# Layer norms split over three engines, high parts multiplied first, and out products moved into the attention's last pairs

## What is computed

```python
for l in range(DEPTH_2):                       # 2 layers
    proj = h @ w_in[l]                         # 8 "in" units
    ...                                        # conv, rotary keys, gating: o_a, o_c
    o_b = blocked_attention(q, k, v, ...)      # 4 heads each, no mask
    o_d = blocked_attention(q_full, k_full, v_d, ...)
    mix = jnp.concatenate([o_a, o_b, o_c, o_d], axis=-1) @ w_out[l]
    h = layer_norm(DEEPNORM_ALPHA * h + mix, ln_mix_g[l], ln_mix_b[l])
    up = depthwise_conv(h @ ffn_w_up[l], ffn_conv_w[l], ffn_conv_b[l])
    f = (jax.nn.silu(up[..., :D_FF]) * up[..., D_FF:]) @ ffn_w_down[l]
    h = layer_norm(DEEPNORM_ALPHA * h + f, ln_ffn_g[l], ln_ffn_b[l])
```

## Time and profile before

| | |
|---|---|
| median of three runs | 2215.06 us |
| profiled execution | 2213.04 us, span 2211.2 us |
| TensorE busy | 2074.5 us, 94% of the span |
| VectorE busy | 1194.1 us, 54% |
| ScalarE busy | 782.5 us, 35% |
| GpSimd busy | 164.4 us, 7% |
| chain that ended last | PE 79%, DMA 10%, DVE 6%, ACT 4%, issue 2% |

### The profile page before, as it was taken

How to read it: one execution, slowest core, us unless ns; L and a number is a source line. 1 busy time by engine, 2 the same in 40 slices (tenths; PEclk the granted TensorE clock), 3 DMA queues, 4 the chain that set the end, 5 groups by cost and what they waited for, 6 DMA issues and landing times.

```text
span 2211.2 us, 24796 instructions
## 1 busy us (share of the span) xinstructions
PE 2074.5 (94%) x10070; PEld 1450.8 (66%) x10070; DVE 1194.1 (54%) x1803; ACT 782.5 (35%) x1191; POOL 164.4 (7%) x120
## 2 busy tenths in 40 slices
PE   6999998999998899889998999999899989999997
PEld 5787787843333333358566888887685567888875
DVE  6455624423332233367775764656677847646565
ACT  4546534221111111154573421222445734212222
POOL 1000000000000000000200110102002001101020
PEclk9999999999999999999999999999999999999999
DMA  5342243479999999932201222233132012232321
GB/s 197 113 156 77 77 152 115 181 286 407 404 413 400 402 412 415 419 111 95 72 1 57 95 95 95 81 110 115 58 114 72 1 58 79 100 104 85 110 96 38
DMA packets 41138, 357.61 MB, mean 162 GB/s; under 512 B 6321, under 2 KB 7513, under 8 KB 13377
## 3 DMA queue, kind: packets, MB, share of 16 engines
q1 hardware_dynamic: 35872, 340.89, 40.6%
q0 software_dynamic: 4288, 10.95, 1.6%
q10 hardware_dynamic: 864, 4.19, 0.5%
HBM read 354.94 MB, written 6.83 MB: 164 GB/s over the span
## 4 chain that ended last, share of the span: by engine, by line
PE 79%; DMA 10%; DVE 6%; ACT 4%; issue 2%; SPq 0%; DVEq 0%; ACTq 0%
PE bank L1078 43%; PE bank L2007 10%; PE bank L443 7%; DMA ring<-in_expert_up_w 4%; PE bank L458 3%; DMA AUX<-in_expert_up_w 3%; PE bank L465 2%; PE bank L1799 2%; DMA H<-in_expert_up_w 2%; PE bank L1784 1%; PE bank L1815 1%; DVE split_weights L1285 1%; PE bank L2032 1%; PE bank L2100 1%; ACT S L1864 1%
## 5 line engine op out<-in xcount | busy, mean ns | idle before, releaser
L1078 PE MATMUL bank<-split_x_high,split_weights 128*128 128x512 f32 x2144 | 668.9, 392 | 22.8 <-DVE split_x_low L1299 14.7
L1078 PEld LDWEIGHTS bank<-split_x_high,split_weights 128*128 128x128 f32 x2144 | 405.5, 189 | 113.1 <-issue 28.7
L1293 ACT ACTIVATE split_weights<-ring 128x2048 fp32r<-128x2048 f32 (+2 forms) x117 | 218.8, 1870 | 554.1 <-PE bank L1078 519.4
L1285 DVE TENSOR_TENSOR split_weights<-ring,split_weights 128x2048 fp32r<-128x2048 f32 (+2 forms) x117 | 265.2, 2267 | 172.1 <-ACT split_weights L1293 172.0
L1078 PE MATMUL bank<-split_products,split_weights 128*128 128x512 f32 x1200 | 332.4, 393 | 4.5 <-DVE split_products L1475 4.5
L1078 PE MATMUL bank<-split_x_low,split_weights 128*128 128x512 f32 x800 | 313.0, 391 | 0.0
L1078 PEld LDWEIGHTS bank<-split_products,split_weights 128*128 128x128 f32 x1200 | 227.6, 190 | 53.8 <-DVE split_products L1475 6.0
L1078 PEld LDWEIGHTS bank<-split_x_low,split_weights 128*128 128x128 f32 x800 | 151.3, 189 | 31.6
L2007 PE MATMUL bank<-split_x_high,split_weights 128*128 128x512 f32 x512 | 163.4, 397 | 6.5 <-DVE split_x_low L2189 6.5
L1056 POOL TENSOR_TENSOR QKVG<-QKVG 128x512 f32<-128x512 f32 x44 | 97.8, 2223 | 791.4 <-DVE QKVG L1489 708.9
L670 DVE SCALAR_TENSOR_TENSOR S<-S,stats,bank 64x512 f32<-64x512 f32 x32 | 23.7, 740 | 222.6 <-ACT S L793 222.6
(11 more groups left out here) (435 smaller groups left out, 2963.9 us busy)
## 6 DMA issues: line engine op xcount, KB each, us to landing
ring<-in_ffn_w_up SPq DMA_DIRECT2D x44, 1024.0 KB, 4.9
ring<-in_w_in SPq DMA_DIRECT2D x24, 1024.0 KB, 4.8
QKVG<-in_expert_gate_w SPq DMA_DIRECT2D x11, 2048.0 KB, 24.4
AUX<-in_expert_up_w SPq DMA_DIRECT2D x11, 2048.0 KB, 29.3
QKVG<-in_expert_down_w SPq DMA_DIRECT2D x11, 2048.0 KB, 20.5
MKV<-in_expert_gate_w SPq DMA_DIRECT2D x11, 2048.0 KB, 25.0
ring<-in_expert_up_w SPq DMA_DIRECT2D x11, 2048.0 KB, 29.5
ring<-in_expert_down_w SPq DMA_DIRECT2D x11, 2048.0 KB, 20.1
```

What stands on the lines that cost most here:

```text
L1078: mm = pe.matmul(acc[:, :], w[:, u, k, m], x, start=first and q == 0, stop=last and q == 2)
L1285: st.tell(dve.tensor_tensor(w[:, 1, 0:ks, 0:nc_], raw_half(g)[:, :, 0:nc_], as_f32(w[:, 0, 0:ks, 0:nc_]), ALU.subtract), wl_done)
L1293: st.tell(act.activation(WHL[g % 2][:, 0, 0:ks, 0:nc_], raw_half(g)[:, :, 0:nc_], ACT.Copy), wh_done)
```

## The change

- **Norm, mean:** ScalarE first writes minus the mean to SBUF (`sum_x`), then its square. GpSimd adds it to chunks 5, 6 and 7. VectorE centres chunk 0 ahead of the variance, chunks 1 and 2 behind the clamp, 3 and 4 between the scalings, each from PSUM as before.
- **Norm, first unit:** `high_first` multiplies both weight halves by a chunk's high part as soon as that is there, and the low part's products one chunk later. Unit 1 (`low_last`) starts with the high weight half and needs the low one only behind 16 products of a tile. Its high half is copied by ScalarE in two pieces, behind chunks 1 and 3, and the bias of X comes four chunks late in place of two.
- **TensorE's filler:** four products of ones into an unused bank follow the statistics of each norm but the last. The feed-forward norm's statistics stand in banks 4 and 5, no longer 0 and 1.
- **Out units:** the first unit's chunks 6 and 7 go ahead of values 14 and 15; its other six follow. Units 1 to 3 finish one tile before the other.
- **Second out unit:** its low half is made behind the attention.

```diff
@@ layer_gpsimd
+            def centred_by_gpsimd(use):
+                pool.wait_ge(ln_mean, 2 * use + 1)
+                for c in range(LN_SPLIT, DC):
+                    st.tell(pool.tensor_tensor(X[:, c, :], X[:, c, :], sum_x[:, :], ALU.add), ln_pool)
@@ layer_tensor
+                def low_last(acc, w, m, g, x, lo):
+                    pe.wait_ge(wh_done, g + 1)
+                    for k in range(DC):
+                        pe.matmul(acc[:, :], w[:, 0, k, m], x(k), start=k == 0, stop=False)
+                        pe.matmul(acc[:, :], w[:, 0, k, m], lo(k), start=False, stop=False)
+                    pe.wait_ge(wl_done, g + 1)
+                    for k in range(DC):
+                        mm = pe.matmul(acc[:, :], w[:, 1, k, m], x(k), start=False, stop=k == DC - 1)
+                    return mm
+                def high_first(accs, w, before, low, done):
+                    def lows(k):
+                        pe.wait_ge(xl_done, before + k + 1)
+                        for i, acc in enumerate(accs):
+                            mm = pe.matmul(acc[:, :], w[:, 0, k, i * P:(i + 1) * P], low[:, k, :], start=False, stop=k == DC - 1)
...
+                    for k in range(DC):
+                        pe.wait_ge(xh_done, before + k + 1)
+                        for i, acc in enumerate(accs):
+                            for u in range(2):
+                                pe.matmul(acc[:, :], w[:, u, k, i * P:(i + 1) * P], XH[:, k, :], start=k == 0 and u == 0, stop=False)
+                        if k:
+                            lows(k - 1)
+                    lows(DC - 1)
@@ the end of the attention
                 def first(kind, p):
+                    if kind == "values" and p >= len(l_pairs) - 2:
+                        out_first(order[p - len(l_pairs) + 2])
...
+                for k in order[2:]:
+                    out_first(k)
+                for m in range(1, N_OUT):
...
+                    for i, acc in enumerate(accs):
+                        for k in order:
+                            mm = three(acc, WHL[g % 2], slice(i * P, (i + 1) * P), k, XH[:, k, :], OL[k], k == order[0], k == order[-1])
+                        mm.then_inc(r_done, 1)
@@ layernorm
+                    for _ in range(idle):
+                        pe.matmul(bank[6][:, :], ones, konst[:, 0:T], start=True, stop=True)
@@ normed, VectorE
-                dve.wait_ge(ln_mean2, use + 1)
-                for c in range(2):
-                    centre(c)
+                dve.wait_ge(ln_mean, 2 * use + 1)
+                for c in range(1):
+                    centred[c] = centre(c)
+                dve.wait_ge(ln_mean, 2 * use + 2)
                 dve.wait_ge(ln_stat, 2 * use + 2)
                 step(dve.scalar_tensor_tensor(rstd[:, :], bank[b][:, :], 1.0 / D, rstd[:, :], ALU.mult, ALU.subtract))
                 st.tell(dve.tensor_scalar(rstd[:, :], rstd[:, :], 0.0, None, ALU.max), ln_vard)
-                for c in range(2, DC):
-                    centre(c)
+                for c in range(len(centred), 3):
+                    centred[c] = centre(c)
                 dve.wait_ge(ln_rstd, use + 1)
                 for c in range(DC):
+                    if c in centred:
+                        st.wait(centred[c])
+                    else:
+                        dve.wait_ge(ln_pool, (DC - LN_SPLIT) * use + c - LN_SPLIT + 1)
                     st.tell(dve.scalar_tensor_tensor(X[:, c, :], X[:, c, :], g(c), rstd[:, :], ALU.mult, ALU.mult), ln_scaled)
...
+                    if c and c + 2 < LN_SPLIT:
+                        centred[c + 2] = centre(c + 2)
@@ normed, ScalarE
-                st.tell(act.activation(rstd[:, :], bank[a][:, :], ACT.Square, scale=1.0 / D), ln_mean2)
+                st.tell(act.activation(sum_x[:, :], bank[a][:, :], ACT.Identity, scale=-1.0 / D), ln_mean)
+                st.wait()
+                st.tell(act.activation(rstd[:, :], sum_x[:, :], ACT.Square), ln_mean)
```

More of the change, by code:

```diff
@@ L1198, in layer_tensor @@
                 pe_pairs(pe, l_cfg, l, first)
[L1200 to L1204 removed]
+                for k in order[2:]:
+                    out_first(k)
+                for m in range(1, N_OUT):
+                    accs = [bank[(2 * m + i) % 4] for i in range(2)]
                     for i in range(2):
@@ L1542, in bias @@
                     st.tell(act.activation(X[:, c, :], X[:, c, :], ACT.Identity, bias=b(c)), ln_ready)
+                if split:
+                    w, raw, half = WHL[unit % 2], raw_half(unit), DC // 2
+                    act.wait_ge(half_landed[unit % 2], 16 * (unit // 2 + 1))
+                    act.wait_ge(*unit_used(unit - 2))
                 for c in range(DC):
@@ L1554, in normed @@
                 if split:
-                    bias(DC - 2)
-                    bias(DC - 1)
+                    for c in range(DC - 4, DC):
+                        bias(c)
             for l in range(L2):
```

115 lines of the change are left out of this document (60 added, 55 removed).

## The result

The changed kernel takes 2191.41 us (median of four runs, 2185.73 to 2193.54) against 2214.80 us for the kernel before (median of four beside them): ratio 0.9883, 95% interval 0.9870 to 0.9896. In a second comparison it took 2189.59 against 2215.79 us (0.9878, 0.9862 to 0.9895). The forecast was 2192.2 us, range 2186 to 2201. The profiled execution took 2189.99 us, its span 2188.2.

The account below looks back on a forecast made before the run. TensorE was taken to bound the second block, the only one touched. Savings of 8.2 + 2.8 + 0.2 + 4.2 + 6.8 + 0.7 = 22.9 us from 2215.06 gave 2192.2 us, range 2186 to 2201.

Parts of the forecast that it names:

- (a): Two mix norms: last out unit finishes its first tile early, leaving one add behind the last product; 1.3 us each.
- (b): Norms: only two centrings between clamp and first scaling, so ScalarE's root releases the scaling; 2.1 us saved.
- (c): Norms: GpSimd's three additions end about as scaling starts, but hold VectorE's clamp; 0.6 us lost in all four norms.
- (d): Norm's next unit, behind first scaling (T): ends at T + 14.0 in place of T + 15.3; 1.3 us saved.
- Final norm: Last norm, only output behind it: 2.1 - 0.6 - 2 x 0.665 = 0.2 us saved, two centrings among its scalings.
- (e): End of attention: six products ahead of each of the last two value steps fill TensorE's holes; 4.2 us, two layers.
- (f): Ahead of attention: second out unit's split leaves VectorE's path to the rotated keys; 3.4 us a layer, 6.8 in all.
- (g): Entry to the second block: first products follow the high part, 0.7 us sooner.
- The clock did not fall while the chunks were fed: Rival, norms' first units: clock falls during the feed, up to 8 us, 2200; chance 0.14 shared with unfilled gaps.
- no spilling: Rival: GpSimd's late additions hold VectorE's scalings, 3.2 us in each of four norms, 2202; chance 0.05.
- the gaps were filled: Rival, attention's end: delayed work makes (e) give nothing, 2196.4; chance 0.14 shared with the clock falling more than once.
- Slower: Rival: TensorE stays at low clock through the first unit of three norms, 24 us, 2216.6; chance 0.01.

Follow-up runs that it names:

- e5: Changed kernel with no GpSimd share, all eight centrings on VectorE (LN_SPLIT = 8): 2197.90 us, ratio 0.9924 to the kernel before.
- e6: Changed kernel with GpSimd's three additions waiting for the clamp in place of the mean: 2197.06 us, ratio 0.9912 to the kernel before.
- e12: Changed kernel with variance and clamp written in place in the statistics' PSUM bank: one run, 2185.68 us.
- e8: Changed kernel with all of the first out unit's products behind the attention, as before: 2194.71 us, ratio 0.9905 to the kernel before.
- e2: Changed kernel with the second out unit's low half made ahead of the rotation of the keys, as before: 2196.23 us, ratio 0.9913.
- e1: Changed kernel without the four filler products behind each norm's statistics: 2194.52 us, ratio 0.9905 to the kernel before.

## Why the prediction was right, point by point

The time and its sign came out, the sum was 4.7 us short in the second block, and the difference of the medians, 23.4 us in one comparison and 26.2 in the other, lies between the sum's 22.9 and the trace's 27.6. The first block alone moves by several us, it ended at 977.8 to 985.6 us over these traces, so that the median came within 0.8 us of the forecast is luck: the second block gained 4.7 us more than was summed.

- **(a) Last tile ahead, 1.3.** From the last product to the `sum_x` product 1.21 us became 0.23, and from there to the third statistic 2.36 became 1.90: 1.44, within its bounds.
- **(b), (c) Centring 2.1 and clamp -0.6.** Mean to first scaling 6.60 us became 4.91: 1.69 against 1.5. The clamp is held for 0.51 us, where I had 0.6; e5, e6 and e12 show by what.
- **(d) Behind the first scaling, 1.3.** The unit ends at T + 13.98, forecast T + 14.0. The term was mis-sized at the mix norms on the side of before. I read T + 15.3 from the first convolution at 1228.73; that row is released by the unit's first tile, three products (0.7 us) before its second, as both take a chunk in turn. By the fourth tile's convolution (1240.29 before, 1234.01 after) less T it is 26.88 against 25.06: 1.8 us, and 1.6 in layer 1, where the low clock lasted 6.8 us in place of 10.2. At the ffn norm, read from ScalarE's copy, which waits for both tiles, 1.3 was nearly right: (b) and (c) take 1.69 of the 2.86 us gained, and 1.2 is left.
- **Final norm 0.2:** 0.55. Mean to first scaling gained 1.7 as elsewhere (forecast 1.5), and the eight scalings with two centrings among them take 6.59 us in place of 5.39, 1.2 where I had 1.33.
- **(e) Gaps, 4.2:** 4.3 by e8.
- **(f) Ahead of the attention, 3.4 a layer:** 3.27, but the step was wrong inside. VectorE did gain 3.3 us (from the first out unit's split, 1078.83 to 1100.31 before, 1082.95 to 1101.13 after). I took that for the gain; what the runs show is 2.4, plus 0.8 for a fall of the clock that was not in the sum, so it is luck that the line came out. TensorE, not VectorE's path alone, sets the attention's start: its wait shrank by 1.63. VectorE's own path had the fall in it too: in e2, with the split ahead and the clock up, it is 20.84 us long against 21.48 before. "Under 5 us" for GpSimd's cosines was 5.05. Three products at 1.28 us would end at 1090.3, not at the 1091.3 of the forecast, and they take 1.7 us each even without the split.
- **(g) Entry 0.7:** the first product comes 0.72 us sooner, 0.50 is left at the first statistic.
- **What the sum left out:** the hole in the feed-forward, behind which the clock fell in before and not in after, 1.5 and 1.6 us: 3.1 of the missing 4.7. Most of the rest is the mix norms, 0.8 us more each than the 3.1 forecast. The change doesn't remove that fall: e2, e8 and e12, which keep its norms and filler, had it. I had read the 10 us table for the stretches of the change and called the rest of the block a mere shift. A fall costs time in stretches that the change doesn't touch, and it can come or go there.
- **Rivals.** The clock did not fall while the chunks were fed (it would without filler, e1, for 0.8 to 1.35 us); no spilling (e6 has its price); the gaps were filled; the clamp did wait. "Slower" needed a clock that stays low for a unit: in e1, with a hole of 4.96 us, 6.8 us was the longest.

## What to carry to other kernels

List every hole of the bounding engine, also those that an edit doesn't touch, and ask of each whether something else is ready to multiply: two tiles' early chunks ahead of either's late ones closed one for 2.7 us a layer. Give GpSimd work only where VectorE reads PSUM, and end it before the first operation with two inputs from SBUF. When two traces are compared, measure by stage from a common instruction, since here an untouched block moved by up to 8 us between executions, and read the last tile of a unit, not the first, for its end.

## What the runs showed of the hardware

- Holes of 2.1 to 2.3 us in dense TensorE work were followed by a fall to 1.2 GHz in some cases and not in others (15 of 22 in the feed-forward, 5 of 8 ahead of the attention), with nothing different in the instructions; one fall cost 0.8 to 1.6 us. What did differ is where the hole began against the raster of the clock's own changes (0.92 to 1.42 with a fall, 0.43 to 0.84 without; 36 holes). Behind holes of 1.5 us or less none was seen in the second block; behind 1.93 us (e6) it fell three times in three, all three at places where the longer holes fell too.
- A VectorE operation with two inputs from SBUF and one that reads one input from SBUF at the double pace (the clamp, 0.43 us) were both held by GpSimd's additions, two scalings by 1.92 us together and the clamp by 0.51; one reading PSUM (0.70) was not. The clamp from SBUF ended 0.28 to 0.29 us behind the addition that was running when it started, in four norms of four. GpSimd's cosine products hold a scaling of the keys in the same way, in both kernels: 1.77 us where its neighbours take 0.75. The Trainium skill's page "VectorE: DVE Perf Modes", section "Why PSUM operands drop a tier", says that an fp32 operand in PSUM loses the double pace, as PSUM has one read port for VectorE. The 0.70 agrees: slower than 0.43 alone, faster than 0.94 held.
- Where the clock stayed up, the stretches of the second block repeat to 0.02 us between two executions of the changed kernel.
